# Another order of VectorE's and ScalarE's work in the down stage of a mixture-of-experts layer

## The reference

```python
h = jax.nn.gelu(jnp.einsum('lkd,ld->lk', u, xb), approximate=False)     # u = expert_u[ib]
return jnp.einsum('lk,lkd->ld', gb * h, expert_v[ib])
```

## Time and profile before

| what | us |
|---|---|
| median of 3 runs | 3954.94 |
| these runs | 3953.03 to 3958.17 |
| the profiled execution's own time | 3948.47 |
| its span | 3946.4 |
| busy in the span: PE, PEld, DVE | 3446.7, 2983.5, 2830.9 |
| busy in the span: ACT, POOL | 1424.7, 1164.6 |

### The profile page before, as it was taken

One profiled execution on the slowest core, in us unless ns is written; L12 is line 12 of the kernel. 1 busy time (PEld: TensorE's weight loads), 2 busy tenths in 40 slices (PEclk: granted clock), 3 DMA queues, 4 the chain that ended last, 5 costly groups with the idle time before them and its releaser, 6 DMA issues.

```text
span 3946.4 us, 46600 instructions
## 1 busy us (share of the span) xinstructions
PE 3446.7 (87%) x18582; PEld 2983.5 (76%) x18582; DVE 2830.9 (72%) x4525; ACT 1424.7 (36%) x1889; POOL 1164.6 (30%) x726
## 2 busy tenths in 40 slices
PE   7999999977778899888889789798888999888887
PEld 5977688867767898666667776687888998676766
DVE  3366533598898995677776587559999995777776
ACT  4324522322224563222223435332224663222222
POOL 0000000167888832333331000002334332333331
PEclk9999999988888999999999899899999999999999
DMA  3211232367778998788886220225778998888884
GB/s 119 85 34 54 70 118 80 115 216 252 252 241 284 306 352 324 287 303 305 305 305 228 75 65 6 91 85 205 241 250 270 363 362 321 314 304 308 304 305 169
DMA packets 373498, 855.56 MB, mean 217 GB/s; under 512 B 22449, under 2 KB 237329, under 8 KB 340130
## 3 DMA queue, kind: packets, MB, share of 16 engines
q1 hardware_dynamic: 299554, 584.12, 42.5%
q0 software_dynamic: 73728, 268.47, 19.5%
HBM read 746.58 MB, written 105.93 MB: 216 GB/s over the span
## 4 chain that ended last, share of the span: by engine, by line
DVE 45%; PE 35%; ACT 10%; issue 5%; DMA 3%; POOL 1%; DVEq 0%; SPq 0%; POOLq 0%; ACTq 0%
PE ps L294 30%; DVE parts L277 12%; DVE xres L1626 7%; ACT parts L269 6%; DVE scr L1609 5%; DVE scr L1689 3%; PE ps L1404 2%; DVE scr L1652 2%; DMA scr<-in_p_rows_u,cst 2%; DVE scr L1586 2%; DVE scr L1590 2%; DVE scr L1584 1%; PE ps L316 1%; DVE scr L1588 1%; DVE scr L1558 1%
## 5 line engine op out<-in xcount | busy, mean ns | idle before, releaser
L294 PE MATMUL ps<-ht_hi,parts 128*128 128x384 f32 (+1 forms) x5008 | 1422.8, 360 | 101.3 <-DVE parts L277 97.1
L294 PEld LDWEIGHTS ps<-ht_hi,parts 128*128 128x128 f32 x5008 | 961.8, 197 | 161.9 <-DVE parts L277 108.9
L277 DVE TENSOR_TENSOR parts<-ring,parts 128x2048 fp32r<-128x2048 f32 (+1 forms) x317 | 740.3, 2336 | 348.9 <-ACT parts L269 348.8
L294 PE MATMUL ps<-ht_lo,parts 128*128 128x384 f32 (+1 forms) x2504 | 892.9, 357 | 0.0
L269 ACT ACTIVATE parts<-ring 128x2048 fp32r<-128x2048 f32 (+1 forms) x317 | 604.4, 1907 | 155.1 <-PE ps L294 137.3
L322 ACT ACTIVATE scr<-ps 128x384 f32<-128x384 f32 (+3 forms) x496 | 243.9, 505 | 1131.9 <-PE ps L294 1069.6
L1404 PE MATMUL ps<-parts,ht_lo 128*128 128x512 f32 x2304 | 563.0, 406 | 91.6 <-DVE parts L277 91.6
L1731 POOL DMA_INDIRECT scr<-in_peer_v,cst x256 | 397.8, 1554 | 798.9 <-DVE xres L1626 699.5
L1731 POOL DMA_INDIRECT scr<-in_p_rows_u,cst x256 | 437.7, 1710 | 660.1 <-DVE scr L1609 473.2
L1404 PEld LDWEIGHTS ps<-parts,ht_lo 128*128 128x128 f32 x2304 | 450.7, 197 | 203.2 <-DVE parts L277 106.7
L1404 PE MATMUL ps<-parts,ht_hi 128*128 128x512 f32 x2304 | 539.5, 392 | 64.5 <-DVE parts L277 57.6
(11 more groups left out here) (227 smaller groups left out, 3183.9 us busy)
## 6 DMA issues: line engine op xcount, KB each, us to landing
ring<-in_peer_u SPq DMA_DIRECT2D x128, 1024.0 KB, 7.1
ring<-in_peer_v SPq DMA_DIRECT2D x128, 1024.0 KB, 4.9
hbuf<-scr SPq DMA_DIRECT2D x128, 384.0 KB, 7.7
gbuf<-scr SPq DMA_DIRECT2D x96, 512.0 KB, 8.9
scr<-gbuf SPq DMA_DIRECT2D x64, 768.0 KB, 6.4
scr<-hbuf SPq DMA_DIRECT2D x64, 768.0 KB, 8.6
ring<-in_w_in SPq DMA_DIRECT2D x35, 1024.0 KB, 5.4
scr<-in_w_ada SPq DMA_DIRECT2D x48, 512.0 KB, 7.5
```

The costliest lines, as they stand in the source:

```text
L277: e.tensor_tensor(lo, slot_view(m)[:, 0:units[m][0]], hi.bitcast(F32), ALU.subtract).then_inc(V.sem, V.up(("lo", m), ("slot", m)))
L294: ins = e.matmul(ps, l, r, start=(i == 0), stop=(i == n - 1))
```

## The change

In `down_act` the table unit is split first and the weights second. In `down_dve` each unit's two products come first, then the unit's low part, then the two low parts of the weights (a new function `weigh_low`, cut out of `weigh_dve`), then the fetched rows. The rows are spread at 25/12 a unit in place of 9/4, so that the last falls to u = 63 instead of u = 58.

```diff
             def down_act(self, e, w):
                 for u in range(NU + 1):
+                    if u:
+                        split_hi(e, w, U[self.tag + "v", u - 1] + 1)
                     if u < NU:
                         self.weigh_act(e, w, u)
-                    if u:
-                        split_hi(e, w, U[self.tag + "v", u - 1] + 1)
...
                         self.weigh_dve(e, w, u)
                     if u:
                         split_lo(e, w, U[tag + "v", u - 1] + 1)
+                    if u < NU:
+                        self.weigh_low(e, w, u)
                     if u >= 2:
-                        for k in range(min(SLOTS, 9 * (u - 2) // 4), min(SLOTS, 9 * (u - 1) // 4)):
+                        for k in range(min(SLOTS, 25 * (u - 2) // 12), min(SLOTS, 25 * (u - 1) // 12)):
                             self.add_row(e, w, k)
...
+
+            def weigh_low(self, e, w, u):
+                for j in range(2):
+                    hv = self.HB[u // 2 % 2][:, (2 * u + j) % 4, :]
                     w.wait_ge(*self.pt("w_high", u, j))
                     e.tensor_tensor(self.Wp[u % 4][:, 1, j, :], hv, self.Wp[u % 4][:, 0, j, :].bitcast(F32),
                                     ALU.subtract).then_inc(V.sem, V.up((self.tag, "weighed", u)))
```

## The result

The changed kernel takes **3757.0 us** (median of 4 runs, 3752.9 to 3758.0) against 3954.8 us for the kernel before: a ratio of 0.950, 95% interval 0.9488 to 0.9512. The forecast was 3753 us, in a range of 3743 to 3795. The profiled execution took 3752.9 us with a span of 3750.8 us, 195.6 us less than the span before.

What follows compares the result with a forecast made beforehand. DVE with its three waits for ACT was taken as the bound, PE at 8.14 us a unit as the next. Second stage -100.2, first -99.1, starts -2.2: -201.5 us, so 3753 us on the median, range 3743 to 3795.

Steps and rivals of the forecast that it cites:

- PE's pace as the new period: Down stages: PE never waits, so a unit takes 8.14 us, against 9.7 and 9.8 us before.
- the sum: Whole kernel: -100.2 - 99.1 - 2.2 = -201.5 us, which gives 3753 us on the median.
- VectorE's work: Down stages: DVE's own work is 6.8 us for a two-row unit, 8.2 with three rows, mean 6.9, under PE's 8.14.
- The three waits: Down stages: DVE's waits for ACT, 0.59 us for each of two weight copies and 1.25 for the unit's high part, are covered.
- slack: Down stages: a unit is ready some 5.7 us after PE finished unit u - 2, PE wants it after 8.14: 2.4 us.
- The clock: Down stages: with no gaps PE's granted clock should hold 1.00, so nothing is added to 8.14 us.
- The stages: Both down stages: second 521.0 us against 621.2, -100.2 us; first 529.7 against 628.8, -99.1 us.
- unit 9: First down stage: DVE's broadcast row comes late, PE stalls 5.7 us before unit 10, plus 1.5 for the clock: 7.2 us.
- The starts: Start of each down stage: first weights complete about 1.1 us sooner, PE waits for them there (3.7 us idle): -2.2 us.
- Transfers: Down stages: 360 GB/s wanted, no cost taken; the rival that they set the pace, 3813 us, worst 3870, had chance 0.12.
- the 12 us that the ring gives: Down stages: a table unit's load has 12 us to land before ACT would take it, 14.4 before PE would stand.

Runs made afterwards that it cites:

- the repetition: The changed kernel run once more with nothing changed, beside the version with the normalization operation at u = 12 on the same chip: 3755.8 us, ratio 0.9491.

## Why the prediction was right

- **PE's pace as the new period.** Taken as 8.14 us from two units that nothing held; measured 8.16, since 0.04 us lies between pairs of units. Over 126 units that is 2.5 us that the sum left out.
- **VectorE's work**, 6.8 us for a two-row unit: with 1.28 us added twice the period was 9.40, so 6.84.
- **The three waits.** Covered as forecast, 1.21 us left behind PE (forecast 1.3), slack 2.5 us (forecast 2.4). The experiments show that all three are covered only by both orders: ScalarE's order takes away one, VectorE's alone takes away none of the time waited.
- **The clock.** 1.00 wherever PE had no gap, as forecast; it was 0.90 in the first two units of the first stage and 0.91 in the two after the gap at unit 10. That the first two units would run 17.79 us as before was luck: in the repetition they took 16.17. And where I read the lower clock after three-row units, I did not say that it had cost nothing; the run with the rows alone shows at most 13 us.
- **The stages.** -99.1 us for the second (forecast -100.2) and -96.2 us (628.76 to 532.54) for the first (forecast -99.1). Most of the first one's difference is the term for **unit 9**: the gap was 7.58 us and the next 72 loads 1.29 us longer, 8.9 in place of 7.2. I had taken the 10.7 us from issue to use of the kernel before. In the faster stage the load, issued at 1615.19, could be used at 1627.81, after 12.6 us, and these 1.9 us more are what the gap has over the 5.7 forecast. The load also left 5.9 us after PE's end of unit 7 and not 5; my rounding up of the sum to 22 us happened to cover that:

```profile
1615.19 0.43 SPq L1118 DMA_DIRECT2D scr<-in_g_mix  x1
...
1627.81 1.23 DVE L1123 SCALAR_TENSOR_TENSOR scr<-scr 128x1024 f32<-128x1024 f32 x1 [10.07 <-DMA scr<-in_g_mix]
```

- **The starts.** PE's wait there fell from 3.7 to 2.6 us, as forecast:

```profile
3214.95 16.16 PEld L1404 LDWEIGHTS ps<-parts,ht_hi 128*128 128x128 f32 x72 [2.57 <-DVE ht_hi L1699]
```

- **Transfers.** Priced at nothing, and in the regular units they cost nothing. A table unit's landing became longer by half (5.0 to 7.5 us), inside the 12 us that the ring gives. The broadcast row above is the one place where a slower landing cost time.
- In all the span fell by 195.6 us where the sum had 201.5. The stages account for 4.0 of the 5.9 us. The rest lies mainly ahead of the first stage, which began 1.0 us later than before although PE's wait there was 1.1 us shorter; other executions of the changed kernel and its variants began it between 1541.9 and 1548.2, so this is scatter that no run here explains. The median fell by 197.8.

## What to carry to other kernels

When two engines hand pieces to each other in turn, read from the timeline which of them has idle time before every piece: the loop is the sum of that engine's work and its waits, however busy a third engine looks. Putting independent work between a request and its answer paid here only once the answering engine took the requests in the order in which they become critical. So change both sides and test each alone: here one gave 31 us and the other 151 of 198. And the price of the new bound can be read ahead of time, in the stretches in which the old one happened to be absent.

## What was not expected of the hardware

Transfers of 4 to 8 KB a partition kept 413 GB/s over 400 us with all 16 DMA engines taken (share 1.02), beside a PE that was busy for 394 of them. And PE's first 72 weight loads after the same gap differ from run to run of one kernel: after 2.57 us of idle at the first stage's start 17.79 us in one execution and 16.17 in another, and after 7.57 us 17.57 and 19.01. Here is that start in the repetition of the changed kernel:

```profile
1544.10 16.17 PEld L1404 LDWEIGHTS ps<-parts,ht_hi 128*128 128x128 f32 x72 [2.57 <-DVE ht_hi L1699]
```

A difference of one or two microseconds behind a gap is therefore no effect of an edit.
